# Block 0 of a two-block transformer kernel: convolution by channel halves, layer-norm sums earlier, layer-norm root on GpSimd

## The chip, the cores and the metric

The kernel runs on one core of a Trainium2 chip. The metric is the device time of one execution in microseconds. The kernel before took 1688.28 us (median of three runs, 1686.38 to 1688.96). All engines of the core work side by side and meet only at semaphores: PE (TensorE) does matmuls and transposes, DVE (VectorE) and ACT (ScalarE) elementwise work, POOL (GpSimd) small work and some DMA issues, SP (SyncE) issues the DMAs that bring the weights.

## The reference, cut to what matters

The model is a first part of two layers (a mixer and a mixture of experts with 16 experts in each) and a second part. The change is all in the mixer of layer 0 (`even_mixer`), on 256 tokens:

```
proj = hm @ w_in                       # q 512, k and v 256, u 512, gate 512 columns
attn = block_attention(rope(rms(q)), k, v)        # 8 heads, 128-query blocks, 512 keys
g = u * sigmoid(gate)                             # 512 channels
g = depthwise_conv(g, conv_w) + conv_b            # 31 taps along the tokens
g = silu(layer_norm(g, ln_g, ln_b))               # mean and variance over the 512 channels
out = concat([attn, g]) @ w_out
```

`layer_norm` multiplies the centred rows by `rsqrt(var + 1e-6)`.

## The kernel before, in words

Weights stream from HBM through a ring of eight 2 MB slots. SP issues one DMA for each chunk and waits, for chunk i, until PE has marked chunk i - 8 as used (`chunks_used`). Each engine has one program, written out by hand; nothing is reordered when it runs.

PE's order in the mixer: the u projection (`to_columns`, four channel tiles of 128, eight matmuls each, banks 4 and 5), transposes of the convolution weights (`cw_ps`), the gate projection (banks 6 and 7), q, own k and v, context k and v, one group of modulation chunks (`ada(1, ...)`), transposes of q and k, and then the attention loop of 16 turns, two blocks of eight heads. In turn n PE does the scores of head n + 2 (`ev_scores`, L2059), the transposes of the probabilities of head n (`ev_transposed`, L2067, which waits for the exponential of head n), the products with the values of head n - 1 (`ev_values`, L2074), and one chunk of the modulation weights on average (`ada`, L1875). In turns 10 and 11 (`LN_AT`) it also sums the convolution's output and its squares over the channels with a matrix of ones (`cv_sums`, L2087), in bank 6.

DVE's order: with both sigmoids of ACT there, it multiplies u by them in two instructions (L1284), then runs the convolution as 124 taps (31 for each of four channel tiles), each one instruction of 128x256 (L1297, L1300): 35 (`TAPS_Q`), 12 more after the context's transposes (`TAPS_KV`), and eight in each turn of the loop until none is left. Tap k of all four tiles comes before tap k + 1. Between them stand the norms and rotations of q and k. In turn n of the loop DVE takes the row maximum of head n (L1387), copies transposed probabilities of the even heads (L1393), copies modulation rows (`ada_rows`, L1202), and in turns 10 to 12 does the mean and the centring (`ln_center`), the variance and its reciprocal (`ln_inverse`), and the scaling (`ln_scale`, L1383). ACT takes the exponentials (L689), the squares of the centred rows, and the square root of the reciprocal (L699), for which it loads another function table and then the exponential's again.

POOL stores the modulation gates of groups 1, 2, 4 and 5 to HBM (`store_gate`) as DVE delivers them. `ada_rows(5)` on DVE waits until groups 2 and 4 are stored. A GpSimd power with exponent -0.5 is used at other places for 128x1 and 128x4 operands (L1033, L1062).

After the loop come the output projection (`ev_out`), the routing of layer 0 and then the experts, whose chunks PE takes from the ring.

Of the kernel before, what the change touches and what calls it, by code (L numbers as in the profile page):

```python
# [12 lines left out]
P = 128  # L13
D = 1024
N = 256
# [106 lines left out]
def build(nc, a):  # L122
    ctx = ExitStack()
    with ctx:
# [70 lines left out]
        cw = at(9848, c=CT, j=34)  # L195
        cwrow = at(8824, d=512)
        grow = at(9336, i=P)
# [136 lines left out]
        def whole(eng, name, j=0):  # L334

            used_up(eng, FIRST[name] + j)
# [10 lines left out]
        def pb(b):  # L347
            return ps[:, b, :]
# [51 lines left out]
        SMALL2 = 9  # L400
        LN_AT = 10
        TAPS_Q, TAPS_KV, TAPS_LOOP = 35, 12, 8
        GO = (WO[0], FS)
# [157 lines left out]
        def _(act):  # L561
# [82 lines left out]

            whole(act, "ev_gate")
            for j in range(2):
                nc.scalar.activation(flat(sg[:, 2 * j:2 * j + 2, :]), pb(6 + j), ACT.Sigmoid).then_inc(sem("cv_gate"), 1)

# [7 lines left out]
            for w, bank in ((0, 2), (1, 3)):  # L656
                if w:
                    whole(act, "ev_kv")
                else:
                    act.wait_ge(sem("own_kv"), 1)  # L660
# [24 lines left out]
            for n in range(NT * NQ):  # L685
                act.wait_ge(sem("ev_max"), n + 1)
                if n >= 2:
                    act.wait_ge(sem("ev_pT_ps"), n - 1)
                nc.scalar.activation(pexp[:, n % 2, :], pb(n % 3), ACT.Exp, bias=sm[:, 64 + n:65 + n],  # L689
                                     accum_out=sm[:, 96 + n:97 + n]).then_inc(sem("ev_p"), 1)  # L690
                if n % 2 == 0 and n >= 2:
                    ev_probs_T(n - 1)

                if n == LN_AT:
                    act.wait_ge(sem("cv_centered"), 1)
                    nc.scalar.activation(flat(csq), flat(cacc), ACT.Square).then_inc(sem("cv_sq"), 1)
                if n == LN_AT + 1:
                    act.wait_ge(sem("inverses"), 3)
                    nc.scalar.activation(lnrow[:, :], lnrow[:, :], ACT.Sqrt).then_inc(sem("roots"), 1)  # L699
            ev_probs_T(NT * NQ - 1)  # L700
# [306 lines left out]
        def _(pool):  # L1007
# [31 lines left out]

            for g in (2, 4, 5):  # L1040
                store_gate(g)
# [108 lines left out]
        def _(dve):  # L1150
# [119 lines left out]

            dve.wait_ge(sem("cw_ps"), 1)
            nc.vector.tensor_copy(flat(cw), ps[:, 2, 0:CT * 34]).then_inc(sem("cw"), 1)

            dve.wait_ge(sem("params_in"), PARAMS * 16)
# [5 lines left out]

            whole(dve, "ev_u")
            for j in range(2):
                dve.wait_ge(sem("cv_gate"), j + 1)
                nc.vector.tensor_tensor(gpad[:, 2 * j:2 * j + 2, edge:edge + N],  # L1284
                                        pb(4 + j).rearrange("p (c n) -> p c n", c=2), sg[:, 2 * j:2 * j + 2, :], ALU.mult)\
                    .then_inc(sem("gpad"), 1)

            taps_left = [(k, c) for k in range(CONVK) for c in range(CT)]
            TAPS, tap_of = len(taps_left), {}

            def taps(n):

                for _ in range(min(n, len(taps_left))):
# [9 lines left out]
                    tap_of[c] = TAPS - len(taps_left)  # L1303

            dve.wait_ge(sem("cw"), 1)
            dve.wait_ge(sem("gpad"), 2)
            taps(TAPS_Q)
# [63 lines left out]
            def ln_center():  # L1371
                dve.wait_ge(sem("cv_sum"), 1)
                link(nc.vector.tensor_scalar(lnrow[:, :], ps[:, 6, 0:N], 1.0 / 512, None, ALU.mult))
                nc.vector.tensor_tensor(cacc, cacc, mu, ALU.subtract).then_inc(sem("cv_centered"), 1)

            def ln_inverse():
                dve.wait_ge(sem("cv_sum"), 2)
                link(nc.vector.tensor_scalar(lnrow[:, :], ps[:, 6, N:2 * N], 1.0 / 512, EPS, ALU.mult, ALU.add))
                nc.vector.reciprocal(lnrow[:, :], lnrow[:, :]).then_inc(sem("inverses"), 1)

# [4 lines left out]
            for n in range(NT * NQ):  # L1385
# [13 lines left out]
                if n == NQ + 1:  # L1399
                    attn_rows(0)  # L1400
                if n == LN_AT:
                    ln_center()
                if n == LN_AT + 1:
                    ln_inverse()
                if n == LN_AT + 2:
                    ln_scale()
# [453 lines left out]
        def _(pe):  # L1860
# [57 lines left out]

            def to_columns(i, rhs, banks):

                for c in range(4):
                    for k in range(KD):
                        last = mm(ps[:, banks[c // 2], N * (c % 2):N * (c % 2 + 1)], slot8(i)[:, k, P * c:P * (c + 1)],
                                  rhs[:, k, :], start=(k == 0), stop=(k == KD - 1))
                return last
# [84 lines left out]

            i = FIRST["ev_u"]
            arrived(pe, i)
            used(to_columns(i, xT, (4, 5)))
# [4 lines left out]
            i = FIRST["ev_gate"]  # L2018
            arrived(pe, i)
            used(to_columns(i, xT, (6, 7)))  # L2020
            i = FIRST["ev_q"]
# [7 lines left out]
            pe.wait_ge(sem("cw"), 1)  # L2029
            kv_rows(2, xT).then_inc(sem("own_kv"), 1)  # L2030
            normed_columns("ctx")
# [46 lines left out]
            def cv_sums(n):  # L2078

                if n == 0:  # L2080
                    pe.wait_ge(sem("conv"), CT * CONVK)
                    pe.wait_ge(sem("cleared"), 3)
                    pe.wait_ge(sem("ev_attn"), 2)
                else:
                    pe.wait_ge(sem("cv_sq"), 1)
                for c in range(CT):
                    last = mm(ps[:, 6, N * n:N * (n + 1)], ones[:, 0:P], (cacc, csq)[n][:, c, :],  # L2087
                              start=(c == 0), stop=(c == CT - 1))
                last.then_inc(sem("cv_sum"), 1)
# [3 lines left out]
            for n in range(NT * NQ):  # L2093
                if n + 2 < NT * NQ:
                    ev_scores(n + 2)
                ev_transposed(n)
                if n:
                    ev_values(n - 1)
                if n % 4 == 0 and n:
                    ada_columns(1 + n // 4, 3)  # L2100
                if n in (LN_AT, LN_AT + 1):
                    cv_sums(n - LN_AT)

# [562 lines left out]
```

## Time and profile before

| what | value |
|---|---|
| runs | 1688.96, 1688.28, 1686.38 us |
| the profiled execution | span 1688.5 us, no other time of its own is given with it |
| PE busy | 1483.4 us (88%) |
| DVE busy | 480.6 us (28%) |
| ACT busy | 350.1 us (21%) |
| POOL busy | 112.1 us (7%) |
| DMA | 562.89 MB, mean 333 GB/s |
| mean granted TensorE clock | 0.961 of full speed |

The span runs from the first to the last instruction. Busy shares are averages over very different stages. The mixer of layer 0 lies between 37 and about 217 us, its attention loop between 110 and 191 us, the routing of layer 0 until 243 us, the experts of layer 0 until some 720 us.

### The profile page before, as it was taken

The numbers are of one execution on the slowest core, as the hardware profiler recorded it, in microseconds if no ns is written. First come the engines' busy times: TensorE is split into PE (matmuls) and PEld (weight loads), VectorE is DVE, ScalarE is ACT, GpSimd is POOL, SyncE is SP. The second block draws the span as 40 slices with busy tenths as digits, with TensorE's granted clock in tenths as the row PEclk, the third lists the DMA queues.
The fourth block names the chain that finished last, engine by engine and source line by source line (L and its number), as shares of the span: only waits on it lengthen the run. The fifth ranks groups of instructions, "written<-read, shape, count | busy, mean of one in ns | idle before, by whom it ended". The sixth has DMA issues, their size and how long they took to land. (4 is left out here: it accounts for less than half of the span.)

```text
span 1688.5 us, 18007 instructions
## 1 busy us (share of the span) xinstructions
PE 1483.4 (88%) x7708; PEld 831.6 (49%) x7708; DVE 480.6 (28%) x732; ACT 350.1 (21%) x523; POOL 112.1 (7%) x109
## 2 busy tenths in 40 slices
PE   4999979789888899789798888978878999999999
PEld 2755642232242243289532322323324867788997
DVE  1487540110100000056600100001003765336453
ACT  1122410000000000043210000000003645544442
POOL 0000000000000000010000000000002044330000
PEclk8999979989989999999899999999999999999999
DMA  9979959999999999995489999999999743334520
GB/s 373 375 316 418 396 199 429 416 402 429 416 428 428 413 409 429 415 392 202 168 364 423 427 429 423 428 428 421 429 427 364 271 168 135 121 128 174 198 100 26
DMA packets 93288, 562.89 MB, mean 333 GB/s; under 512 B 8048, under 2 KB 9448, under 8 KB 53670
## 3 DMA queue, kind: packets, MB, share of 16 engines
q1 hardware_dynamic: 89504, 551.77, 80.5%
q0 software_dynamic: 2384, 9.42, 1.6%
q8 instruction: 51, 0.84, 0.2%
q10 hardware_dynamic: 1334, 0.75, 0.2%
q14 instruction: 15, 0.12, 0.0%
HBM read 558.74 MB, written 3.17 MB: 333 GB/s over the span
## 5 line engine op out<-in xcount | busy, mean ns | idle before, releaser
L2211 PE MATMUL ps<-ring,scratch 128*32 128x512 f32 x2048 | 439.0, 609 | 63.0 <-DMA ring<-in_moe_w_up 29.6
L2211 PEld LDWEIGHTS ps<-ring,scratch 128*32 128x32 f32 x2048 | 130.7, 112 | 358.2 <-issue 351.1
L2190 PE MATMUL ps<-ring,scratch 128*32 128x512 f32 x1024 | 206.5, 607 | 28.2 <-DMA ring<-in_moe_w_down 28.2
L1930 PE MATMUL ps<-ring_parts,scratch_parts 128*128 128x512 f32 x656 | 187.0, 402 | 4.9 <-DVE xT_parts L1192 1.4
L1930 PE MATMUL ps<-scratch_parts,ring_parts 128*128 128x256 f32 x704 | 146.5, 281 | 0.0
L1930 PEld LDWEIGHTS ps<-ring_parts,scratch_parts 128*128 128x128 f32 x656 | 122.2, 189 | 33.4 <-DVE xT_parts L1192 1.6
L2190 PEld LDWEIGHTS ps<-ring,scratch 128*32 128x32 f32 x1024 | 50.6, 111 | 159.8 <-issue 109.9
L610 ACT ACTIVATE ring_parts<-ring 128x2048 fp32r<-128x2048 f32 x56 | 106.3, 1917 | 93.1 <-PE ps L1930 86.7
L461 DVE TENSOR_TENSOR ring_parts<-ring,ring_parts 128x2048 fp32r<-128x2048 f32 x46 | 105.7, 2298 | 54.9 <-ACT ring_parts L610 53.7
L1930 PEld LDWEIGHTS ps<-scratch_parts,ring_parts 128*128 128x128 f32 x704 | 116.4, 189 | 0.3
L1523 DVE TENSOR_TENSOR scratch<-ps,gate_bc 128x512 f32<-128x512 f32 x16 | 11.1, 692 | 256.8 <-PE ps L2190 256.8
L1930 PE MATMUL ps<-xT_parts,ring_parts 128*128 128x256 f32 x288 | 82.2, 286 | 1.3 <-DVE xT_parts L1183 1.3
L2219 PE MATMUL ps<-scratch,rows 128*128 128x128 f32 (+1 forms) x256 | 66.6, 421 | 14.1 <-DVE scratch L1552 5.7
L2219 PEld LDWEIGHTS ps<-scratch,rows 128*128 128x128 f32 x256 | 61.5, 327 | 32.1 <-issue 31.0
L1512 DVE TENSOR_TENSOR scratch<-scratch,ps 128x1024 f32<-128x1024 f32 x8 | 9.8, 1221 | 236.7 <-PE ps L2211 236.7
L1915 PE MATMUL ps<-ring,xT 128*128 128x512 f32 x160 | 72.9, 616 | 2.5 <-DVE xT L1171 2.5
L746 ACT ACTIVATE scratch<-ps,mod_cols,scale_cols 128x128 f32<-128x128 f32 x32 | 12.9, 453 | 276.9 <-PE ps L2219 276.9
L1930 PE MATMUL ps<-ring_parts,xT_parts 128*128 128x512 f32 x160 | 62.9, 393 | 0.0
L1508 DVE SCALAR_TENSOR_TENSOR scratch<-ps,cst,scratch 128x256 f32<-128x256 f32 x8 | 3.9, 483 | 186.9 <-ACT scratch L750 186.9
L1875 PE MATMUL ps<-ring,silu_c 128*32 128x512 f32 x384 | 50.0, 656 | 7.8 <-issue 6.9
L758 ACT ACTIVATE scratch<-ps 128x512 f32<-128x512 f32 x8 | 4.8, 597 | 246.7 <-PE ps L2245 246.7
L1930 PEld LDWEIGHTS ps<-xT_parts,ring_parts 128*128 128x128 f32 x288 | 54.2, 188 | 1.8 <-issue 1.5
(394 smaller groups left out, 1574.0 us busy)
## 6 DMA issues: line engine op xcount, KB each, us to landing
ring<-in_moe_w_gate SPq DMA_DIRECT2D x64, 2048.0 KB, 26.2
ring<-in_moe_w_up SPq DMA_DIRECT2D x64, 2048.0 KB, 15.6
ring<-in_moe_w_down SPq DMA_DIRECT2D x64, 2048.0 KB, 27.1
ring<-in_ada_w SPq DMA_DIRECT2D x24, 2048.0 KB, 14.0
ring<-in_mlp_w SPq DMA_DIRECT2D x16, 2048.0 KB, 8.5
ring<-in_sc_w_in SPq DMA_DIRECT2D x6, 2048.0 KB, 21.2
ring<-in_w_in SPq DMA_DIRECT2D x6, 2048.0 KB, 20.0
ring<-in_xattn_wkv SPq DMA_DIRECT2D x4, 2048.0 KB, 27.4
```

The lines of the kernel that those rows point to most:

```text
L461: ops.tensor_tensor(lo, w, hi.bitcast(F32), ALU.subtract).then_inc(sem("w_split"), 1)
L610: nc.scalar.activation(hi, w, ACT.Copy).then_inc(sem("w_high"), 1)
L746: last = nc.scalar.activation(xsT[:, k, :], ps[:, GATHER[b], P * (k % 2):P * (k % 2 + 1)], ACT.Identity, scale=scale[:, k:k + 1], bias=shi ...
L758: nc.scalar.activation(flat(hT[:, 4:8, :]), pb(7), ACT.Copy).then_inc(sem("mo_hT_act"), 1)
L1512: nc.vector.tensor_tensor(hid, hid, ps[:, 2:4, :].rearrange("p b f -> p (b f)"), ALU.mult)\
L1523: nc.vector.tensor_tensor(ym[:, 512 * j:512 * j + 512], pb(4 + j), gate_bc[:, 512 * j:512 * j + 512], ALU.mult).then_inc(sem("mo_ym"), 1)
L1875: last = mm(ps[32 * j:32 * j + 32, bank, :], lhs, rhs, start=(c == k == 0), stop=(c == 3 and k == 1))
L1915: last = mm(ps[:, banks[t], col:col + width], lhs[:, k, P * t:P * (t + 1)], slot8(i)[:, k, 0:width], start=(k == 0), stop=(k == KD - 1))
L1930: last = mm(out, lhs[x], rhs[y], start=start and n == 0, stop=stop and n == 2)
L2190: last = mm(ps[32 * j:32 * j + 32, banks[half], :], src[:, k, CAP * j:CAP * (j + 1)], w[:, e, col:col + 512], start=(k == 0), stop=(k == K ...
L2211: last = mm(ps[32 * j:32 * j + 32, banks[half], :], src[:, k, CAP * j:CAP * (j + 1)], w[e][:, 0, col:col + 512], start=(k == 0), stop=(k = ...
L2219: last = mm(ps[:, GATHER[b], P * (k % 2):P * (k % 2 + 1)], run_slice(rows[:, t, :], k), onehot[:, t, bass.ds(g * P, P)], start=(t == 0), s ...
```

## The change

The u and gate projections are done by channel halves in the order u first half, gate first half, transposes of the convolution weights, u second half, gate second half (`two_columns`). ACT takes the sigmoid of the first half once that half is there, DVE gates it, takes 40 taps of the first two channel tiles (`TAPS_FIRST`), gates the second half, and goes on with 30 and 14 taps; taps now run through the first two tiles before the last two. The ring slot of the u chunk is marked as used after its second half. The mean's sums move to turn 5 of PE's loop, into bank 7, the squares' sums to turn 10. DVE centres in its turn 8, writes variance plus epsilon in its turn 12 (without the reciprocal) and scales in its turn 14. The root and the reciprocal become one GpSimd power of 128x256 elements with exponent -0.5, placed between two gate stores. The convolution's raw weights get another place in SBUF.

```diff
-        LN_AT = 10
-        TAPS_Q, TAPS_KV, TAPS_LOOP = 35, 12, 8
+        TAPS_FIRST, TAPS_Q, TAPS_KV, TAPS_LOOP = 40, 30, 14, 8
+        MEAN_AT, CENTER_AT, SQUARE_AT, VAR_AT, SCALE_AT = 5, 8, 9, 10, 12
...
-            for g in (2, 4, 5):
+            store_gate(2)
+            pool.wait_ge(sem("inverses"), 3)
+            nc.gpsimd.tensor_tensor(lnrow[:, :], lnrow[:, :], mhalf[:, 0:1].broadcast_to([P, N]), ALU.pow)\
+                .then_inc(sem("roots"), 1)
+            for g in (4, 5):
                 store_gate(g)
...
-                if n == LN_AT + 1:
-                    act.wait_ge(sem("inverses"), 3)
-                    nc.scalar.activation(lnrow[:, :], lnrow[:, :], ACT.Sqrt).then_inc(sem("roots"), 1)
...
-            taps_left = [(k, c) for k in range(CONVK) for c in range(CT)]
+            taps_left = [(k, 2 * j + c) for j in range(2) for k in range(CONVK) for c in range(2)]
...
+            gated(0)
...
+            taps(TAPS_FIRST)
+            gated(1)
...
-            def ln_inverse():
+            def ln_var():
                 dve.wait_ge(sem("cv_sum"), 2)
-                link(nc.vector.tensor_scalar(lnrow[:, :], ps[:, 6, N:2 * N], 1.0 / 512, EPS, ALU.mult, ALU.add))
-                nc.vector.reciprocal(lnrow[:, :], lnrow[:, :]).then_inc(sem("inverses"), 1)
+                nc.vector.tensor_scalar(lnrow[:, :], ps[:, 6, N:2 * N], 1.0 / 512, EPS, ALU.mult, ALU.add)\
+                    .then_inc(sem("inverses"), 1)
...
-                if n == LN_AT:
+                if n == CENTER_AT:
                     ln_center()
-                if n == LN_AT + 1:
-                    ln_inverse()
-                if n == LN_AT + 2:
+                if n == VAR_AT + 2:
+                    ln_var()
+                if n == SCALE_AT + 2:
                     ln_scale()
...
+            def two_columns(i, half, rhs, bank):
+                for c in range(2 * half, 2 * half + 2):
...
+            two_columns(u, 0, xT, 4).then_inc(sem("ev_part"), 1)
+            arrived(pe, gate)
+            two_columns(gate, 0, xT, 6).then_inc(sem("ev_part"), 1)
...
+            used(two_columns(u, 1, xT, 5))
+            used(two_columns(gate, 1, xT, 7))
...
+                if n == NQ + 1:
+                    pe.wait_ge(sem("cv_centered"), 1)
...
-                if n in (LN_AT, LN_AT + 1):
-                    cv_sums(n - LN_AT)
+                if n == MEAN_AT:
+                    cv_sums(0)
+                if n == VAR_AT:
+                    cv_sums(1)
```

## Rows read from the trace of the kernel before

**Rows 1.** Stages: window and length in us, busy us (count) by engine, clock, DMA share, GB/s.
```profile
37.20:98.50 61.30, 60.39 (x248) 46.32 (x251) 30.02 (x68) 10.65 (x23) 1.89 (x4) 0.96 0.82 319
...
121.10:191.10 70.00, 69.76 (x504) 35.26 (x500) 43.27 (x91) 22.40 (x43) 1.95 (x5) 1.00 1.02 415
...
226.30:243.00 16.70, 9.78 (x46) 5.55 (x48) 9.87 (x25) 1.68 (x3) 0.00 (x0) 0.57 0.27 82
243.00:820.00 577.00, 507.92 (x2546) 241.69 (x2542) 97.29 (x132) 66.94 (x93) 12.47 (x19) 0.97 0.96 394
```

**Rows 2.** Timeline of SP's DMA issues, 205 to 245 us: start us, us, what.
```profile
243.01 2.08 SPq L496 DMA_DIRECT2D ring<-in_moe_w_up  x2
```

**Rows 3.** Timeline of PE, turns 10 to 15 and the first transposes after them.
```profile
160.71 1.95 PE L2087 MATMUL ps<-scratch,ones 128*128 128x256 f32 x8
...
184.98 0.66 PE L2067 MATMUL ps<-cst,scratch 128*128 128x128 f32 x4
185.47 1.00 PE L2074 MATMUL ps<-scratch 128*128 128x64 f32 x8
186.41 3.64 PE L1875 MATMUL ps<-ring,silu_c 128*32 128x512 f32 x32
...
192.17 1.09 PE L2115 MATMUL ps<-cst,xT 128*128 128x128 f32 x8 [1.09 <-DVE xT L1362]
```

**Rows 4.** Timeline of DVE, turns 11 to 15 and the last modulation rows.
```profile
169.66 0.42 DVE L1378 TENSOR_SCALAR ln_row<-ps 128x256 f32<-128x256 f32 x1 [4.09 <-PE ps L2087]
...
173.26 0.69 DVE L1202 COPY scratch<-ps 128x512 f32<-128x512 f32 x1 [0.84 <-PE ps L1875]
173.87 1.22 DVE L1383 TENSOR_TENSOR scratch<-scratch,ln_row 128x1024 f32<-128x1024 f32 x1
...
177.67 0.69 DVE L1387 TENSOR_REDUCE small<-ps 128x1 f32<-128x512 f32 x1 [0.29 <-PE ps L2059]
...
190.12 0.69 DVE L1202 COPY scratch<-ps 128x512 f32<-128x512 f32 x1 [7.89 <-PE ps L1875]
```

**Rows 5.** Groups of POOL by shape: shapes xcount | busy us, mean ns | idle us.
```profile
L1033 POOL TENSOR_TENSOR rstd<-ms,mhalf 128x1 f32<-128x1 f32 x18 | 11.9, 660 | 1.5
...
L1121 POOL TENSOR_TENSOR scratch<-scratch,small 128x512 f32<-128x512 f32 x2 | 2.1, 1042 | 0.2
L1062 POOL TENSOR_TENSOR small<-small,mhalf 128x4 f32<-128x4 f32 x2 | 2.1, 1040 | 0.2
```

**Rows 6.** All instructions of L1033: ns min/median/max, first and last start us.
```profile
L1033 POOL TENSOR_TENSOR rstd<-ms,mhalf x18: 539/552/2467, 17.9 to 1506.8; 128x1 f32<-128x1 f32 x18
```

**Rows 7.** Timeline of ACT, the exponential of turn 15.
```profile
178.75 0.68 ACT L689 ACTIVATE scratch<-ps,small 128x512 f32<-128x512 f32 x1
179.32 0.20 ACT L689 ACTIVATION_READ_ACCUMULATOR scratch<-ps,small 128x1 f32 x1
```

**Rows 8.** Timeline of PE, turns 0 and 1.
```profile
115.18 1.12 PE L2067 MATMUL ps<-cst,scratch 128*128 128x128 f32 x4 [2.05 <-ACT scratch L689]
...
117.83 3.50 PE L1875 MATMUL ps<-ring,silu_c 128*32 128x512 f32 x16
```

**Rows 9.** The stretch at the lower clock inside it, columns as in rows 1.
```profile
114.23:121.06 6.83, 5.88 (x28) 3.13 (x28) 6.83 (x18) 2.05 (x5) 0.09 (x1) 0.50 1.02 420
```

**Rows 10.** Timeline of POOL, storing and loading a modulation gate.
```profile
113.76 0.56 POOL L1024 DMA_DIRECT2D gate_bc<-gate_scratch  x1 [5.07 <-DMA gate_scratch<-scratch]
```

**Rows 11.** Timeline of DVE, taps before the loop and the first head norm.
```profile
71.75 12.36 DVE L1297 SCALAR_TENSOR_TENSOR scratch<-scratch 128x256 f32<-128x256 f32 x31
...
85.84 4.84 DVE L1297 SCALAR_TENSOR_TENSOR scratch<-scratch 128x256 f32<-128x256 f32 x12
91.53 1.49 DVE L1316 TENSOR_TENSOR rows<-scratch 128x1280 f32<-128x1280 f32 x1 [0.85 <-ACT scratch L666]
```

**Rows 12.** SP's issues of L471, 53 to 75 us: starts, and time to landing.
```profile
L471 SPq DMA_DIRECT2D ring<-in_ada_w x2: 368/368/368, 53.9 to 68.3; - x2
...
DMA to landing us min/median/max: 15.5/20.2/24.9
```

More of the change, by code:

```diff
@@ L195, in build @@
         cw = at(9848, c=CT, j=34)
-        cwrow = at(8824, d=512)
+        cwrow = at(5632, d=512)
         grow = at(9336, i=P)
@@ L643, in _ @@
             act.dma_start(glam[:, :], a["cst_i"]).then_inc(sem("first_params_in"), 16)
-            whole(act, "ev_gate")
             for j in range(2):
+                if j:
+                    whole(act, "ev_gate")
+                else:
+                    act.wait_ge(sem("ev_part"), 2)
                 nc.scalar.activation(flat(sg[:, 2 * j:2 * j + 2, :]), pb(6 + j), ACT.Sigmoid).then_inc(sem("cv_gate"), 1)
@@ L659, in _ @@
                 else:
-                    act.wait_ge(sem("own_kv"), 1)
+                    act.wait_ge(sem("ev_part"), 3)
                 for t in range(NT):
@@ L692, in _ @@
                     ev_probs_T(n - 1)
-                if n == LN_AT:
+                if n == SQUARE_AT:
                     act.wait_ge(sem("cv_centered"), 1)
                     nc.scalar.activation(flat(csq), flat(cacc), ACT.Square).then_inc(sem("cv_sq"), 1)
-                if n == LN_AT + 1:
-                    act.wait_ge(sem("inverses"), 3)
-                    nc.scalar.activation(lnrow[:, :], lnrow[:, :], ACT.Sqrt).then_inc(sem("roots"), 1)
             ev_probs_T(NT * NQ - 1)
@@ L1269, in _ @@
             normed("ctx", ctx_rows, ctx_rows)
-            dve.wait_ge(sem("cw_ps"), 1)
-            nc.vector.tensor_copy(flat(cw), ps[:, 2, 0:CT * 34]).then_inc(sem("cw"), 1)
             dve.wait_ge(sem("params_in"), PARAMS * 16)
@@ L1279, in _, with gated @@
             link(nc.vector.memset(gpad[:, :, edge + N:PADW], 0.0))
-            whole(dve, "ev_u")
-            for j in range(2):
+            def gated(j):
+                if j:
+                    whole(dve, "ev_u")
+                else:
+                    dve.wait_ge(sem("ev_part"), 1)
                 dve.wait_ge(sem("cv_gate"), j + 1)
@@ L1303, in taps @@
                     tap_of[c] = TAPS - len(taps_left)
+            gated(0)
+            dve.wait_ge(sem("cw_ps"), 1)
+            nc.vector.tensor_copy(flat(cw), ps[:, 2, 0:CT * 34]).then_inc(sem("cw"), 1)
             dve.wait_ge(sem("cw"), 1)
+            dve.wait_ge(sem("gpad"), 1)
+            taps(TAPS_FIRST)
+            gated(1)
             dve.wait_ge(sem("gpad"), 2)
@@ L1372, in ln_center @@
                 dve.wait_ge(sem("cv_sum"), 1)
-                link(nc.vector.tensor_scalar(lnrow[:, :], ps[:, 6, 0:N], 1.0 / 512, None, ALU.mult))
+                link(nc.vector.tensor_scalar(lnrow[:, :], ps[:, 7, 0:N], 1.0 / 512, None, ALU.mult))
                 nc.vector.tensor_tensor(cacc, cacc, mu, ALU.subtract).then_inc(sem("cv_centered"), 1)
-            def ln_inverse():
+            def ln_var():
                 dve.wait_ge(sem("cv_sum"), 2)
-                link(nc.vector.tensor_scalar(lnrow[:, :], ps[:, 6, N:2 * N], 1.0 / 512, EPS, ALU.mult, ALU.add))
-                nc.vector.reciprocal(lnrow[:, :], lnrow[:, :]).then_inc(sem("inverses"), 1)
+                nc.vector.tensor_scalar(lnrow[:, :], ps[:, 6, N:2 * N], 1.0 / 512, EPS, ALU.mult, ALU.add)\
+                    .then_inc(sem("inverses"), 1)
             def ln_scale():
@@ L1400, in _ @@
                     attn_rows(0)
-                if n == LN_AT:
+                if n == CENTER_AT:
                     ln_center()
-                if n == LN_AT + 1:
-                    ln_inverse()
-                if n == LN_AT + 2:
+                if n == VAR_AT + 2:
+                    ln_var()
+                if n == SCALE_AT + 2:
                     ln_scale()
@@ L1917, in to_rows @@
                 return last
-            def to_columns(i, rhs, banks):
-                for c in range(4):
+            def two_columns(i, half, rhs, bank):
+                for c in range(2 * half, 2 * half + 2):
                     for k in range(KD):
-                        last = mm(ps[:, banks[c // 2], N * (c % 2):N * (c % 2 + 1)], slot8(i)[:, k, P * c:P * (c + 1)],
+                        last = mm(ps[:, bank, N * (c % 2):N * (c % 2 + 1)], slot8(i)[:, k, P * c:P * (c + 1)],
                                   rhs[:, k, :], start=(k == 0), stop=(k == KD - 1))
@@ L2009, in kv_rows @@
                 return last
-            i = FIRST["ev_u"]
-            arrived(pe, i)
-            used(to_columns(i, xT, (4, 5)))
+            u, gate = FIRST["ev_u"], FIRST["ev_gate"]
+            arrived(pe, u)
+            two_columns(u, 0, xT, 4).then_inc(sem("ev_part"), 1)
+            arrived(pe, gate)
+            two_columns(gate, 0, xT, 6).then_inc(sem("ev_part"), 1)
             pe.wait_ge(sem("params_in"), PARAMS * 16)
@@ L2017, in _ @@
             last.then_inc(sem("cw_ps"), 1)
-            i = FIRST["ev_gate"]
-            arrived(pe, i)
-            used(to_columns(i, xT, (6, 7)))
+            used(two_columns(u, 1, xT, 5))
+            used(two_columns(gate, 1, xT, 7))
             i = FIRST["ev_q"]
@@ L2029, in _ @@
             pe.wait_ge(sem("cw"), 1)
-            kv_rows(2, xT).then_inc(sem("own_kv"), 1)
+            kv_rows(2, xT).then_inc(sem("ev_part"), 1)
             normed_columns("ctx")
@@ L2082, in cv_sums @@
                     pe.wait_ge(sem("cleared"), 3)
+                    pe.wait_ge(sem("cv_gate"), 2)
+                else:
                     pe.wait_ge(sem("ev_attn"), 2)
-                else:
                     pe.wait_ge(sem("cv_sq"), 1)
                 for c in range(CT):
-                    last = mm(ps[:, 6, N * n:N * (n + 1)], ones[:, 0:P], (cacc, csq)[n][:, c, :],
+                    last = mm(ps[:, 7 - n, N * n:N * (n + 1)], ones[:, 0:P], (cacc, csq)[n][:, c, :],
                               start=(c == 0), stop=(c == CT - 1))
```

## Prediction

> **What bounds the kernel now.** I read the stages first [rows 1]. From 37.2 us to the end of the attention loop PE is the bound: 60.39 of 61.30 us busy before the loop, 69.76 of 70.00 in turns 2 to 15. The memory system is busy too (share 1.02 in the loop) but it is not what PE waits for, or PE would show idle time. In the routing, from 226.3 to 243.0 us, the DMA share falls to 0.27: the ring is full, and SP issues the next chunk only at 243.01 [rows 2], when the first expert chunk has been used. From there to 820 us the share is 0.96. So the moment at which PE reaches the experts starts a stretch that the DMA paces, and whatever the mixer gains or loses before 243 us passes to the end one for one. The question is thus when the loop ends, and the place to look is its last turn: transposes of head 15 at 184.98, two modulation chunks at 186.41, DVE's copy of them at 190.12, the next transposes at 192.17 [rows 3, 4].
>
> **Front part, by halves.** PE does the same matmuls in another order, so its sum stays. The gate's first half is ready where u was ready before, at about 53.9 us (SP's release of the u slot, [rows 12]). I allow 2.0 us for the sigmoid, the gating and the weights' copy (no row; an estimate), so taps start near 55.9. Before, the 31 taps from 71.75 on and four more ahead of them came first then. One tap costs 12.36/31 = 0.40 us [rows 11]. 40 taps end at 55.9 + 16.0 = 71.9, gating again 0.7, 30 taps end at 84.6, the context's copies (85.84 - 84.11 = 1.7) at 86.3, 14 taps at 91.9. The head norm started at 91.53 [rows 11], so it comes 0.4 us later. The last thing that PE takes from this chain is the transposes of k, and they stand behind eight transposes of q, some 1.1 us by the eight in [rows 3]; that covers it. I cost it at 0, at most 0.4. The earlier slot release is lost: u's slot comes free after 61 us instead of 53.9. Its DMA landed 24.9 us after its issue, the next one's 15.5 [rows 12]: it sat in a queue, so 7 us of delay are hidden. Cost 0; without that cover, up to 7.
>
> **The loop's taps.** 84 taps are done before the loop instead of 47, so 40 are left, five turns, instead of 77, ten turns. DVE has 5 x 3.2 us less to do in turns 5 to 9. PE was busy throughout these turns [rows 1], so this is worth 0.2 us at most, PE's idle time there (70.00 - 69.76).
>
> **The sums.** Two groups of eight matmuls, 1.95 us each [rows 3]. One moves from turn 11 to turn 5, turns 5 to 11 run 1.9 us later, turn 12 is back in place. Its input, all 124 taps, is ready at the end of DVE's turn 4; ahead of the sums PE transposes head 5, and for that DVE must have taken the maximum of head 5, which comes after those taps: no wait. PE's wait for the centring in turn 9 and DVE's two centring instructions (0.42 + 1.22) before the maximum of head 9 may cost 0.3 us. Behind that wait stand the values of head 8 and the rest of PE's turn. The ACT table changes go, off the path: their end left PE 0.2 us idle, which is the 0.2 already counted. Together: -0.2 to +1, I take +0.3.
>
> **The power on GpSimd.** This is the term that matters. The trace shows the same operation at 128x1 and at 128x4 only. 128x1 takes 0.552 us in the median [rows 6] (the mean, 0.660, has an outlier of 2.467 in it), 128x4 1.040 [rows 5]. Three more elements per partition cost 0.488 us, 0.163 each. 256 elements: 0.552 + 255 x 0.163 = 42.0 us. Other ends: if a power cost in bulk what a multiply costs, 128x512 in 1.042 us [rows 5], it would be 0.9 us with the power's start; if the whole of the 128x4 instruction scaled (0.26 for each element), 66.6 us. The bulk rate isn't shown: a loop over many elements could overlap what a loop of four can't. I take 42, an estimate from the two power sizes, as they are the only rows of this operation, and keep 0.9 and 66.6 as the ends.
>
> Who waits. `ada_rows(4)` starts at 173.26 and takes 0.69, `ln_var` behind it 0.42 like L1378 [rows 4]; with 0.3 from the sums and 0.1 for the semaphore the power starts at 174.8 and ends at 216.8. DVE reaches `ln_scale` in its turn 14, about 178, and stands there. Queued behind it on DVE are the maximum of head 15, the copy of head 14's transposed probabilities, `ada_rows(5)` and `attn_rows(1)`. ACT's exponential of head 15 waits for the maximum, PE's transposes of head 15 for the exponential, and behind them stand the values of head 14 and the last two modulation chunks. After the power: scaling 1.22, maximum 0.69 [rows 4], exponential 0.68 + 0.20 [rows 7], some 0.2 of semaphores: PE transposes at 219.8 instead of 184.98 [rows 3]. That is 34.8 us. In general the delay is the power's length less 7.2 us: up to 7.2 us DVE, ACT and PE hide it.
>
> POOL's queue: `store_gate(4)` stands behind the power, is issued at 216.8, and takes about a microsecond to issue and 5.07 us to land [rows 10], 223. `ada_rows(5)` waits for it; it comes after 3.64 us of chunks [rows 3] that start near 222 at the lower clock, so near 227. Hidden. `store_gate(5)` isn't late relative to the rest. SP: the chunks waiting for the last two modulation slots are issued late, too, but by the same 35 us; the ring is full at the routing as before, since chunk 37 had 16.7 us to spare [rows 1].
>
> **The clock.** A PE that stood idle for 35 us resumes at the lower level. A shorter idle time, in turns 0 and 1, was followed by 6.83 us at a granted clock of 0.50 (1.2 GHz), with 5.88 us of PE work in it [rows 9]; the transposes took 1.12 us instead of 0.66, 16 modulation matmuls 3.50 where 32 took 3.64 at full clock [rows 3, 8]. Half of 5.9 is 2.9 us lost. Between 0 (the clock stays) and 5.3 (the 3.64 us of chunks and 1.66 us of transposes and values at half speed).
>
> **Sum.** 0 (front) + 0.3 (sums) are in the power's start; 34.8 + 2.9 = 37.7 us. The profiled execution gives only its span, 1688.5 us, which is 0.2 above the median of the runs, 1688.3; the trace holds nothing outside the span that the change touches. 1688.3 + 37.7 = 1726 us.
>
> **Rivals.**
> A. The power is cheap in bulk. Where: at `ln_scale`. It decides from 7.2 us, some 27 ns an element: with a shorter power nothing waits, and the time is 1688.3 + 0.3, about 1688.5, not slower. For it: POOL's multiply does an element in 2 ns [rows 5]. Against it: the two power sizes differ by 163 ns an element. The Trainium skill, GPSIMD Engine Reference, section 3.1 (Elementwise, side-by-side cycle accounting), has about 2.6 cycles of 1.2 GHz an element for two-input work, whatever the operation; by that the power would take about 0.6 us, an estimate, and this rival would hold. The trace agrees with the rule for the multiply and not for the power. 11%.
> B. The power costs half as much in bulk, 82 ns an element, 21 us: delay 21 - 7.2 + 2.9 = 17, time 1705. For it: the 128x1 instruction takes 0.552 us, more than three elements' worth, so start and rate can't be parted exactly from two sizes. 17%.
> C. Dearer, up to 66.6 us: 59.4 + 2.9 = 62, time 1750. 4%.
> D. Faster: DVE's relief in turns 5 to 9 and earlier taps gain something. It would need more than 3.4 us; PE's idle time is 0.9 us before the loop and 0.24 in it [rows 1], and the 2.05 us in turn 1 [rows 8] stay, as eight taps stay there. The low clock behind them (2.9 us) would have to go as well. 1684. 2%.
> That the change doesn't do what it says: the taps would have to end later than PE's turn 5; with 40 left they can't.
>
> **How the numbers follow.** The forecast, 1726, holds with 66% (a power of 35 to 48 us, 1719 to 1732). About 0.2% (3.4 us) is what a measurement of this kernel tells from no change. Slower by more needs a power over 10.6 us, or 8 with the clock's loss: 66 + 17 + 4 = 87%, less 1 for the cheap end of B, is 86. Within it: 11% and the 1. Faster: 2%. The range leaves out A, D, the cheap half of B's spread below 1700, and C: 1700 to 1734.
>
> **What would show it.** One POOL instruction of L1042 or near it, TENSOR_TENSOR on ln_row 128x256, of about 42 us from 175 us on; DVE idle before the scaling (38 us) with POOL as what ended it; PE idle before the transposes of head 15 for 34 us; a lower clock for some 7 us afterwards; the first expert chunks issued near 281 instead of 243.01 us; taps starting at 56 us and ending in turn 4; turn 12 of the loop in its old place. Wrong it is if the power takes under 10 us: then only the front and the loop are left, and the time is that of before. A delay in the front, if the head norm starts over a microsecond late and the loop with it, would be the other miss.

## The result, and the profile after

The changed kernel takes 1723.74 us (median of four runs, 1721.8 to 1724.46), the kernel before 1687.86 beside it (four runs, 1686.38 to 1688.96): 35.9 us slower, ratio 1.0218, 95% interval 1.0204 to 1.0231, which is 34 to 39 us. The prediction was 1726, range 1700 to 1734. The profiled execution took 1723.58 us, its span is 1721.8, so 1.8 us lie outside the span; the span of before is 1688.5.

In the page's busy times only POOL's moved by much, from 112.1 us:

```profile
PE 1478.5 (86%) x7708; PEld 831.3 (48%) x7708; DVE 478.7 (28%) x731; ACT 347.4 (20%) x520; POOL 152.8 (9%) x110
```

The 40.7 us are one new instruction of 41.16 us; the other rows of POOL differ by fractions of a microsecond. What the view of its line has on it, with who waited:

```profile
L1042 POOL TENSOR_TENSOR ln_row<-ln_row,mhalf x1: 41158/41158/41158, 173.3 to 173.3; 128x256 f32<-128x256 f32 x1
its engine sat idle before it (us, times) until:
  DVE ln_row L1389: 39.8, 1
who waited for it (us, times):
  DVE scratch L1394: 38.6, 1
```

The timeline of POOL, DVE, ACT and PE behind it (start us, us, what, in brackets the idle time before and what ended it), lines that answer to [rows 3, 4, 7]:

```profile
214.46 1.03 POOL L1019 DMA_DIRECT2D gate_scratch<-scratch  x2
214.52 1.22 DVE L1394 TENSOR_TENSOR scratch<-scratch,ln_row 128x1024 f32<-128x1024 f32 x1 [38.57 <-POOL ln_row L1042]
215.67 0.68 DVE L1398 TENSOR_REDUCE small<-ps 128x1 f32<-128x512 f32 x1
...
216.38 0.69 ACT L692 ACTIVATE scratch<-ps,small 128x512 f32<-128x512 f32 x1 [38.96 <-DVE small L1398]
...
217.22 1.12 PE L2079 MATMUL ps<-cst,scratch 128*128 128x128 f32 x4 [33.59 <-ACT scratch L692]
218.12 1.81 PE L2086 MATMUL ps<-scratch 128*128 128x64 f32 x8
...
219.86 5.02 PE L1886 MATMUL ps<-ring,silu_c 128*32 128x512 f32 x32
...
224.81 1.10 PE L2086 MATMUL ps<-scratch 128*128 128x64 f32 x8
224.96 0.69 DVE L1206 COPY scratch<-ps 128x512 f32<-128x512 f32 x1 [8.01 <-PE ps L1886]
...
227.00 1.09 PE L2132 MATMUL ps<-cst,xT 128*128 128x128 f32 x8 [1.09 <-DVE xT L1373]
```

The chain is power, scaling, maximum of head 15, exponential, transposes. DVE stood idle for 38.57 us, but PE's 33.59 is what counts, since PE had work left when DVE stopped. DVE's copy at 224.96 shows 8.01 us of idle before PE as in [rows 4] (7.89): the gate's store behind the power was in time.

The clock and the memory system in the same stretch (columns as in rows 1; PE idle, the stretch of low clock, from there to the first expert chunk, the experts):

```profile
183.60:217.20 33.60, 0.02 (x3) 0.00 (x0) 2.42 (x3) 0.78 (x2) 31.89 (x3) 0.57 0.35 144
188.56:222.69 34.13, 5.47 (x28) 3.32 (x32) 2.42 (x3) 5.07 (x7) 26.93 (x3) 0.50 0.19 81
222.70:277.80 55.10, 42.79 (x234) 32.14 (x228) 32.75 (x59) 17.03 (x26) 4.77 (x9) 0.85 0.52 184
277.80:820.00 542.20, 471.45 (x2354) 211.95 (x2351) 74.77 (x105) 56.18 (x86) 12.43 (x19) 0.97 0.99 408
```

The clock stood at the lower level from 188.56 to 222.69, 5.47 us of work with it. SP's issue of the first chunk that waits for an expert's is the line that answers to [rows 2]:

```profile
277.78 9.45 SPq L496 DMA_DIRECT2D ring<-in_moe_w_up  x4
```

277.78 - 243.01 = 34.8 us late. That is PE's idle time (33.6) and the loss at the low clock (2.6, worked out below), less the 1.2 us by which this execution was ahead when its loop began, which would be 35.0. The spans differ by 33.3; 1.5 us are given back among the experts of layer 0. The reason was not tested; the two executions have low-clock stretches of different length there.

The front part (DVE, then SP's release of the u slot):

```profile
56.06 15.13 DVE L1302 SCALAR_TENSOR_TENSOR scratch<-scratch 128x256 f32<-128x256 f32 x38
...
85.37 5.62 DVE L1302 SCALAR_TENSOR_TENSOR scratch<-scratch 128x256 f32<-128x256 f32 x14
...
90.92 1.48 DVE L1327 TENSOR_TENSOR rows<-scratch 128x1280 f32<-128x1280 f32 x1
...
60.20 7.28 SPq L471 DMA_DIRECT2D ring<-in_ada_w  x2
```

Taps start at 56 us, the head norm at 90.92. No idle time stands before it any more ([rows 11] had 0.85): DVE has just become the later one there. PE's loop began 1.2 us earlier than in the profile before, because the low-clock stretch in its first projection was shorter in this execution: the granted clock from 37 to 46 us is 0.81, in the profile before 0.69. One later profile of a kernel with the new front (the scaling after the loop and the store first, below) has 0.69 there, too, and its loop begins where the one before began, at 108.75 instead of 108.72 us. There the new front cost PE nothing.

It is not free in every execution, though. In six of the nine profiles with the new front PE's first projection ended 1.0 to 1.8 us earlier than here, and PE then waited 0.74 to 1.34 us before the transposes of k. None of the four profiles with the old front has that wait. From the front part alone:

```profile
105.84 0.66 PE L2058 MATMUL ps<-cst,scratch 128*128 128x128 f32 x4 [0.74 <-DVE scratch L1337]
```

### The profile page after: what moved, and what is told of

Its sections match the earlier page's. It is cut to its first block and busy times, and to the rows that moved or that the text cites. A ratio compares the mean times of both kernels' runs of the same rounds, so it can differ in the third digit from the quotient of the medians.

```text
span 1721.8 us, 18008 instructions
## 1 busy us (share of the span) xinstructions
PE 1478.5 (86%) x7708; PEld 831.3 (48%) x7708; DVE 478.7 (28%) x731; ACT 347.4 (20%) x520; POOL 152.8 (9%) x110
## 5 line engine op out<-in xcount | busy, mean ns | idle before, releaser
L2207 PEld LDWEIGHTS ps<-ring,scratch 128*32 128x32 f32 x1024 | 50.3, 111 | 161.9 <-issue 108.0
L1941 PE MATMUL ps<-ring_parts,rows_parts 128*128 128x512 f32 x160 | 52.7, 398 | 1.6 <-DVE ring_parts L461 1.4
```

The lines of the kernel that those rows point to most:

```text
L1941: last = mm(out, lhs[x], rhs[y], start=start and n == 0, stop=stop and n == 2)
L2207: last = mm(ps[32 * j:32 * j + 32, banks[half], :], src[:, k, CAP * j:CAP * (j + 1)], w[:, e, col:col + 512], start=(k == 0), stop=(k == K ...
```

## The experiments

Each time is compared with the kernel before, run beside it on the same chip. Its medians are 1685.6 us (for the power alone, the sizes, 32 and 96 columns), 1686.0 (root on ACT, front alone, 128x2, no taps first) and 1685.6 (scaling after the loop, store first, no taps first on the kernel before). Its single executions lie between 1681.6 and 1691.2 us. Ratio and interval are those of the comparison; they differ from the quotient of the two medians by up to 0.15%, 2.5 us, and where that matters both are given. The code is cut, and relative to the kernel that the heading names.

**The power alone (on the kernel before).**

```diff
-                if n == LN_AT + 1:
-                    act.wait_ge(sem("inverses"), 3)
-                    nc.scalar.activation(lnrow[:, :], lnrow[:, :], ACT.Sqrt).then_inc(sem("roots"), 1)
...
+            pool.wait_ge(sem("inverses"), 3)
+            nc.gpsimd.tensor_tensor(lnrow[:, :], lnrow[:, :], mhalf[:, 0:1].broadcast_to([P, N]), ALU.pow)\
+                .then_inc(sem("roots"), 1)
...
-                nc.vector.reciprocal(lnrow[:, :], lnrow[:, :]).then_inc(sem("inverses"), 1)
```

> The kernel before with one part of the change alone: reciprocal and square root become the GpSimd power of 128x256, all else stays (sums in turns 10 and 11, scaling in DVE's turn 12, 47 taps before the loop). Theory 1 (the power is the whole cost, and the delay is its length less what the place of the scaling hides): the power starts near 170.2 us, ends near 211.4; scaling, maximum of head 13 and exponential follow, PE transposes head 13 at 214.4 instead of 177.56, 36.8 us late, and 2.9 us go to the lower clock: 1687.9 + 39.7 = 1727.6 us. Theory 2 (halves and earlier sums cost or gain something of their own, and the power only part of the 36 us): clearly below 1724 or above 1731.

Measured 1727.8 us (1726.92 to 1728.84), ratio 1.0242, interval 1.0217 to 1.0267. The power runs 41.16 us. This kernel scales in DVE's turn 12, like the one before, so PE's wait stands before the transposes of head 13:

```profile
207.88 1.23 DVE L1384 TENSOR_TENSOR scratch<-scratch,ln_row 128x1024 f32<-128x1024 f32 x1 [37.41 <-POOL ln_row L1039]
...
210.57 1.11 PE L2068 MATMUL ps<-cst,scratch 128*128 128x128 f32 x4 [36.81 <-ACT scratch L689]
```

One part of the change makes its whole loss. By the waits it loses a little more here: with the scaling two turns later the changed kernel hides 41.16 - 33.59 = 7.6 us of the power, here it is 41.16 - 36.81 = 4.4. The intervals of the two ratios overlap, so the times alone don't show that difference.

**Without the power (on the changed kernel): root back on ACT.**

```diff
-            pool.wait_ge(sem("inverses"), 3)
-            nc.gpsimd.tensor_tensor(lnrow[:, :], lnrow[:, :], mhalf[:, 0:1].broadcast_to([P, N]), ALU.pow)\
-                .then_inc(sem("roots"), 1)
...
+                nc.vector.reciprocal(lnrow[:, :], lnrow[:, :]).then_inc(sem("inverses"), 1)
...
+                if n == VAR_AT + 3:
+                    act.wait_ge(sem("inverses"), 3)
+                    nc.scalar.activation(lnrow[:, :], lnrow[:, :], ACT.Sqrt).then_inc(sem("roots"), 1)
```

> The changed kernel with the root back where it was: reciprocal on DVE in turn 12, square root on ACT in turn 13, scaling in turn 14; halves, taps and sums as changed. Theory 1 (the power is the whole loss, and the rest is hidden behind PE): 1687.9 us, between 1686.5 and 1689. Theory 2 (halves and early sums gain, and the power hid it): under 1684.5. Theory 3 (they cost): over 1691.

Measured 1687.86 us (12 runs), ratio 1.0005, interval 0.9992 to 1.0019. Halves, taps and early sums together are worth nothing that can be told from zero (-1.3 to +3.2 us). Undoing the power gives the 36 us back.

**The front part alone (on the kernel before): halves, 40, 30 and 14 taps; sums in turns 10 and 11.**

```diff
-        TAPS_Q, TAPS_KV, TAPS_LOOP = 35, 12, 8
+        TAPS_FIRST, TAPS_Q, TAPS_KV, TAPS_LOOP = 40, 30, 14, 8
...
+            two_columns(u, 0, xT, 4).then_inc(sem("ev_part"), 1)
+            arrived(pe, gate)
+            two_columns(gate, 0, xT, 6).then_inc(sem("ev_part"), 1)
...
```

> The kernel before with the front part of the change alone: projections and gating by halves, 40, 30 and 14 taps; sums, root and scaling as before. Theory 1: DVE has nothing to do for 15 us in turns 5 to 9 and PE takes no notice, 1687.9 +- 1 us. Theory 2 (the later release of the u slot or the head norm costs): up to 7 us more, 1689 to 1695.

Measured 1685.53 us, ratio 0.9991, interval 0.9977 to 1.0005. The 1687.9 +- 1 written down stood on a kernel before at 1687.9; it ran at 1686.0 here. From 120 to 186 us, the kernel before, then this one:

```profile
120.00:186.00 66.00, 65.78 (x466) 33.01 (x458) 43.67 (x93) 17.34 (x37) 1.95 (x4) 0.99 1.02 415
```

```profile
120.00:186.00 66.00, 65.78 (x478) 33.52 (x480) 27.77 (x53) 19.91 (x39) 1.94 (x4) 1.00 1.02 415
```

DVE has 27.77 us of work instead of 43.67, and PE is as full as before, 65.78 us. An engine that wasn't awaited was given less to do.

**Sizes of the power (instructions added to the kernel before, on data of no use).**

```diff
+            tv = sil[:, :, :].rearrange("p k v -> p (k v)")
+            link(nc.gpsimd.memset(tv, 1.5))
+            for k in (1, 2, 4, 8, 16, 64, 128, 256):
+                link(nc.gpsimd.tensor_tensor(tv[:, 0:k], tv[:, 0:k], mhalf[:, 0:1].broadcast_to([P, k]), ALU.pow))
+            link(nc.gpsimd.tensor_tensor(tv[0:16, 0:256], tv[0:16, 0:256], mhalf[0:16, 0:1].broadcast_to([16, 256]), ALU.pow))
+            link(nc.gpsimd.tensor_tensor(tv, tv, mhalf[:, 0:1].broadcast_to([P, 256]), ALU.mult))
+            link(nc.gpsimd.tensor_tensor(tv, tv, ones[:, :], ALU.pow))
```

> The kernel before with powers of 1, 2, 4, 8, 16, 64, 128 and 256 elements per partition, a power of 16 partitions x 256, a multiply and a power with a full second operand, all on GpSimd behind the norm of the routing, on data that is of no use elsewhere. Theory 1 (a fixed part and a constant rate): 0.4 + 0.16 us for each element, so 0.55, 0.7, 1.04, 1.7, 2.95, 10.6, 20.8 and 41.2 us, and the 16 partitions take as long as 128, since each partition has its own lane. Theory 2 (time goes with all elements): the 16-partition power takes an eighth, 5 us. The multiply near 0.6 us. The stretch of 79 us of powers stands ahead of POOL's gate load, which DVE waits for, so the time is some 70 to 80 us longer.

The groups of POOL by shape (columns as in rows 5):

```profile
L1050 POOL TENSOR_TENSOR silu_c<-silu_c,ones 128x256 f32<-128x256 f32 x1 | 41.2, 41231 | 0.1
L1047 POOL TENSOR_TENSOR silu_c<-silu_c,mhalf 128x256 f32<-128x256 f32 x1 | 41.1, 41115 | 0.1
L1048 POOL TENSOR_TENSOR silu_c<-silu_c,mhalf 16x256 f32<-16x256 f32 x1 | 41.1, 41105 | 0.1
L1047 POOL TENSOR_TENSOR silu_c<-silu_c,mhalf 128x128 f32<-128x128 f32 x1 | 20.7, 20725 | 0.1
L1047 POOL TENSOR_TENSOR silu_c<-silu_c,mhalf 128x64 f32<-128x64 f32 x1 | 10.5, 10519 | 0.1
L1047 POOL TENSOR_TENSOR silu_c<-silu_c,mhalf 128x16 f32<-128x16 f32 x1 | 2.9, 2893 | 0.1
L1047 POOL TENSOR_TENSOR silu_c<-silu_c,mhalf 128x8 f32<-128x8 f32 x1 | 1.6, 1634 | 0.1
L1047 POOL TENSOR_TENSOR silu_c<-silu_c,mhalf 128x4 f32<-128x4 f32 x1 | 1.0, 1012 | 0.1
L1047 POOL TENSOR_TENSOR silu_c<-silu_c,mhalf 128x1 f32<-128x1 f32 x1 | 1.0, 993 | 0.1
L1047 POOL TENSOR_TENSOR silu_c<-silu_c,mhalf 128x2 f32<-128x2 f32 x1 | 0.7, 708 | 0.1
...
L1049 POOL TENSOR_TENSOR silu_c<-silu_c,mhalf 128x256 f32<-128x256 f32 x1 | 0.6, 612 | 0.1
```

From 128 to 256 elements it is 20.390/128 = 0.159 us an element, from 4 to 16 it is 1.881/12 = 0.157: a straight line from 2 elements to 256, with nothing saved in bulk. The single power of one element is off it, 0.993 us where 0.55 was expected; it was the first of the row, and [rows 6] has one such reading, too (2.467 against a median of 0.552). What makes them long wasn't tried. 16 partitions take as long as 128. A power with exponent 1.0, given as a full operand, takes as long as one with -0.5. The multiply of the same shape takes 0.612 us, one 67th. Theory 1 holds. The whole kernel, run once, took 1841.6 us, 156 more, where 70 to 80 were written down: that sum left the 16-partition power and the last power out, 82 us of the 163.

**A shorter power (on the changed kernel): 32 and 96 columns.**

```diff
-            nc.gpsimd.tensor_tensor(lnrow[:, :], lnrow[:, :], mhalf[:, 0:1].broadcast_to([P, N]), ALU.pow)
+            nc.gpsimd.tensor_tensor(lnrow[:, 0:96], lnrow[:, 0:96], mhalf[:, 0:1].broadcast_to([P, 96]), ALU.pow)
```

> The changed kernel with the power on 32 of the 256 columns only; the other columns keep the variance in place of its inverse root. Theory 1: the power takes 0.39 + 32 x 0.159 = 5.5 us, under the 7.2 us that are hidden; DVE may wait 1 to 2 us in turn 14, PE nowhere: 1687 to 1689 us. Theory 2 (a wait on GpSimd costs as such, or the store behind it): above 1691.

> The changed kernel with the power on 96 of the 256 columns only; the other columns keep the variance. Theory 1: 0.39 + 96 x 0.159 = 15.7 us, less 7.2 hidden is 8.5 us of delay at PE's transposes of head 15; if PE's clock falls in this shorter idle time another 2.6: 1696 to 1699 us. Theory 2 (delay in proportion to the power's length, nothing hidden): 15.7/41.2 of 36 us, 13.7: 1701.6 us.

Both kernels leave the root out for the other columns, so what they compute is not the layer, and only their times are of use. 32 columns: 1685.71 us, ratio 0.9999 (0.9986 to 1.0011); PE did not wait for the scaling at all. The median is below the 1687 to 1689 written down, as the kernel before is here at 1685.6 and not at 1687.9. Its power and DVE's wait:

```profile
174.20 5.45 POOL L1042 TENSOR_TENSOR ln_row<-ln_row,mhalf 128x32 f32<-128x32 f32 x1 [39.77 <-DVE ln_row L1389]
179.68 1.23 DVE L1394 TENSOR_TENSOR scratch<-scratch,ln_row 128x1024 f32<-128x1024 f32 x1 [2.87 <-POOL ln_row L1042]
```

96 columns: 1699.33 us, just above the 1696 to 1699 written down. The ratio, 1.0069 (1.0044 to 1.0094), makes that 11.6 us (7 to 16), the two medians 13.8. Its timeline:

```profile
173.34 15.66 POOL L1042 TENSOR_TENSOR ln_row<-ln_row,mhalf 128x96 f32<-128x96 f32 x1 [39.77 <-DVE ln_row L1389]
...
191.72 1.11 PE L2079 MATMUL ps<-cst,scratch 128*128 128x128 f32 x4 [8.10 <-ACT scratch L692]
192.63 1.80 PE L2086 MATMUL ps<-scratch 128*128 128x64 f32 x8
194.36 5.98 PE L1886 MATMUL ps<-ring,silu_c 128*32 128x512 f32 x32
```

15.66 - 8.10 = 7.6 us hidden, the same as with the long power. So the delay is the power's length less 7.6 us. To it come 3.6 us of low clock (5.98 for the chunks where [rows 3] has 3.64, and 1.2 in the two before them), where I had put 2.6. 8.1 + 3.6 = 11.7 lies well within the interval. A delay in proportion to the length would be a wait of 12.8 us (33.59 x 15.66/41.16); the time alone couldn't tell it from theory 1, PE's wait of 8.10 rules it out.

**Where the scaling stands (on the changed kernel).** First the scaling behind `attn_rows(1)`, then also the store of gate 4 ahead of the power.

```diff
-                if n == SCALE_AT + 2:
-                    ln_scale()
...
             attn_rows(1)
+            ln_scale()
```

> The changed kernel, power kept, with the scaling moved from DVE's turn 14 to behind the attention's last rows (after the loop). Theory 1 (who waits, as in the prediction): the loop itself runs through, heads 14 and 15 lose nothing, but the store of gate 4 stands behind the power on POOL, and DVE's last modulation rows wait for it: issue at 214.5, landed some 6 us later, 220.5; attention rows and scaling until 223.5; then Silu on ACT and the split, first product of the output projection near 227 instead of 230.5 in the changed kernel: 1719 to 1723 us, hardly better. Theory 2 (only the maximum of head 15 waits on the power): the loop's end is not touched by POOL, and the time falls to about 1714.

> As the run with the scaling after the loop, and the store of gate 4 put ahead of the power on POOL. Theory 1: nothing but the scaling waits now: the power ends near 215.5, scaling, Silu, high and low parts until some 220, where the first product of the output projection starts (195.3 in the kernel before), 25 us late, and 3 us of clock: 1714 to 1717 us. Theory 2 (the store was no wait): the same time as the run with the scaling after the loop.

1718.44 us (ratio 1.0189, 1.0174 to 1.0203) and 1716.85 us (1.0176, 1.0161 to 1.0192). DVE and PE of the first, then PE of the second:

```profile
217.55 0.69 DVE L1206 COPY scratch<-ps 128x512 f32<-128x512 f32 x1 [35.90 <-DMA gate_scratch<-scratch]
...
219.19 1.97 PE L2131 MATMUL ps<-cst,xT 128*128 128x128 f32 x8 [28.68 <-DVE xT L1373]
```

```profile
221.22 0.77 PE L1940 MATMUL ps<-ring_parts,scratch_parts 128*128 128x512 f32 x1 [26.03 <-DVE scratch_parts L1430]
```

In the first the loop runs through, and the wait that takes the place of the old one is the gate's store behind the power in POOL's queue. The prediction had this wait, and had it hidden behind PE's late chunks; here nothing hides it. The store had landed 2.2 us after its issue at 215.31, not the 5 to 6 that I took from [rows 10], so this run is just under the range written down. In the second only the scaling waits, and 1716.85 is within its range. The intervals of the two overlap; that the store was a wait is shown by the idle time of 35.90 us and its releaser, not by the 1.6 us between the medians. Why the second gains so little can be read: PE's wait fell from 28.7 to 26.0 us only, as the power began 1.1 us later behind the store and Silu and the split follow the scaling.

**The root as a GpSimd power of 128x2 (on the changed kernel).**

```diff
+            nc.gpsimd.tensor_tensor(lnrow[:, 0:NT], lnrow[:, 0:NT], mhalf[:, :], ALU.pow).then_inc(sem("roots"), 1)
...
+                        for c in range(CT):
+                            last = mm(ps[:, 6, N + t:N + t + 1], csq[:, c, P * t:P * (t + 1)], ones[:, 0:1],
+                                      start=(c == 0), stop=(c == CT - 1))
...
+                for t in range(NT):
+                    last = mm(ps[:, 6, P * t:P * (t + 1)], lnrow[:, t:t + 1].broadcast_to([P, P]), ident, start=True, stop=True)
```

> The changed kernel with the root still a GpSimd power, but of 128x2: the squares' sums come out with the tokens on the partitions, the power is taken there, and two matmuls with the identity spread the 256 values over all partitions as a row in PSUM, which the scaling reads in DVE's turn 15. Theory 1 (elements per partition set the power's length): 0.7 us for the power, no wait: 1687 to 1689 us, as with the root on ACT. Theory 2 (GpSimd in the chain costs as such): over 1691.

Measured 1689.93 us, ratio 1.0021 (1.0007 to 1.0034): the 36 us are gone, but it is 3.5 us slower than before, above the range, under the 1691 of theory 2. The power takes 0.72 us and DVE doesn't wait for it. PE has 0.6 us more to do in turn 13, the two matmuls. A part of the rest may lie in the clock. In the profiled execution 16 one-column matmuls at 159.84 were followed by 3.4 us at the lower level (162.6 to 166.0), which cost 1.8 us, half of it here:

```profile
161.67 2.78 PE L1885 MATMUL ps<-ring,silu_c 128*32 128x512 f32 x16
```

instead of 1.92. Whether the one-column matmuls bring it about wasn't tried, and 0.6 and 1.8 don't make up 3.5 us; the cause stays open.

**No taps in DVE's first two turns.** On the kernel with the root on ACT, and on the kernel before (with ten taps a turn).

```diff
-                taps(TAPS_LOOP)
+                if n >= 2:
+                    taps(TAPS_LOOP)
```

> The kernel of the run with the root on ACT, and the 40 taps left moved from DVE's turns 0 to 4 to turns 2 to 6, the mean's sums from turn 5 to 7. In turns 0 and 1 PE waited 2.05 and 0.74 us for exponentials that stood behind taps, and ran 6.8 us at the lower clock afterwards. Theory 1 (these waits are DVE's taps, and the clock follows the waits): up to 2.8 us less, and up to 2.9 more if the clock holds: 1682 to 1685.5 us. Theory 2 (the clock falls for the sparse work before the loop whatever turn 1 does): only the 2 us of waits, some of it again to the low clock, 1686 to 1687. Theory 3: nothing, other waits take their place.

> The kernel before, with no taps in DVE's turns 0 and 1 and ten a turn from turn 2 on (80 places for the 77 left), sums, root and projections as they were. Theory 1 (the gain of the run without taps in the first turns needs the halves): ten taps are 4.0 us, with maximum and copy 5.0 us a turn on the average, over PE's 4.8: what turns 0 and 1 gain is lost in turns 2 to 9: 1685 to 1688 us where the kernel before has 1686. Theory 2 (it comes from the two turns alone): 3 to 5 us faster, as with the halves.

1684.64 us, ratio 0.9977 (0.9963 to 0.9991), and 1682.38 us, ratio 0.9978 (0.9968 to 0.9989). By the ratios both are some 3.8 us faster than the kernel before (1.5 to 6 us), by the medians 1.3 and 3.2. They are the only two versions whose whole interval lies below 1. The gain needs no halves; theory 1 of the second run falls. From 107 to 120 us, the kernel before, then the second:

```profile
107.00:120.00 13.00, 9.82 (x48) 5.69 (x50) 11.06 (x27) 5.19 (x10) 1.80 (x3) 0.78 1.01 422
```

```profile
107.00:120.00 13.00, 12.26 (x80) 5.49 (x76) 11.27 (x25) 4.11 (x10) 0.56 (x1) 1.00 1.01 417
```

PE's wait of 2.05 us in turn 1 [rows 8] is gone and the clock stays up, 80 matmuls are done in the time of 48. In the first of the two the profile shows a low-clock stretch of 6.83 us later, from 188.55; in the second none up to 221 us, and short waits of PE (0.24 to 0.62 us) in its ten-tap turns. That the clock follows this wait is not shown by that. In two of the other profiles (32 columns, and the scaling after the loop) the clock fell ahead of turn 1, at 108.0 and 107.8 us, some 2 us after PE's wait of 1.3 us before the transposes of k, and stayed low for 13.6 us. Of the first:

```profile
108.02:121.66 13.64, 13.03 (x42) 5.39 (x38) 12.59 (x29) 2.87 (x8) 0.56 (x1) 0.50 1.01 419
```

## Why the prediction was right, point by point

**Bound and transmission.** Right within 1.5 us. A delay of 33.6 us in turn 15 plus the clock's share appears as 34.8 us at the first expert chunk and as 33.3 us of span.

**The power.** The term that carried the sum: 42.0 us taken, 41.16 measured. The line through 128x1 and 128x4 had a slope of 0.163 against 0.159. The reservation that bulk might be cheaper, on which rivals A and B lived, is answered by the sizes: it isn't. That the line hit so well has some luck in it. It was drawn 64 times as far as its two points, and a tenth of a microsecond in the first of them is 8 us in the end: with the mean of 128x1 (0.660) in place of the median (0.552) the same sum gives 33 us, and with the single 0.993 that the sizes run has for 128x1 it would give 5. The median of 18 readings was the right choice; a check at one larger size is what makes it safe.

Rival A's mechanism was right in itself (the run with 32 columns: nothing on PE waits), its price was wrong: 0.9 us against 41.16. The Trainium skill (GPSIMD Engine Reference, section 3.1) gives its 2.6 cycles an element for `tensor_tensor` as what reading two inputs costs at least, and the operation that it measured is an add. By that a two-input instruction of 128x256 takes 0.55 us, an estimate; the multiply's 0.612 us is near it and the power's 41.16 isn't. The prediction's "whatever the operation" is more than the page says.

**What hides it.** 7.2 us taken, 7.6 measured twice. From the power's end to the transposes it is 217.22 - 214.49 = 2.7 us where 3.0 was summed. The power's start, 174.8 in the sum and 173.33 in the profile, is earlier mostly for the 1.2 us by which this execution was ahead, and that shifts the end of what hides it as well.

**The clock.** 2.9 us taken. From the transposes of head 15 to the last values' start it is 224.81 - 217.22 = 7.59 us against 189.98 - 184.98 = 5.0 in the kernel before, 2.6. With the power of 96 columns it was 3.6, so this term isn't a constant. After the transposes began, the low level lasted 5.5 us (to 222.69) where some 7 were expected.

**Sum.** 34.8 + 2.9 = 37.7 predicted, 35.9 measured. The traces account for 1.5 of the 1.8 between them: 0.8 is the power's length, 0.4 what hides it and 0.3 the clock. The measured 35.9 is itself known to some 2 us only, so this split is finer than the times can confirm; against the medians of the kernel before in the later comparisons, 1685.6 to 1686.0, it would be near 38. The base of the sum compared a span, 1688.5, with times of whole executions, which are 1.8 us longer; the median that was used is not touched by that.

**Front, taps, sums.** Costed at 0, 0.2 at most, and 0.3. Root on ACT and halves alone give 1.0005 and 0.9991, both with zero inside. The later slot release (60.20 instead of 53.9) was hidden. The front's "at most 0.4" is too small: the eight transposes of q don't cover the later head norm when PE arrives early, and PE waited up to 1.34 us. The times are too coarse to show it. The sums cost nothing: in the profile with the same clock in the first projection as before the transposes of head 15 come at 184.66 instead of 184.98, though the loop began 0.03 later, so +0.3 has the wrong sign.

**Rival D** was right that this change leaves turn 1 as it is (2.06 us of wait in its profile). What I put at 2% as out of reach (the 2.05 us and the clock behind them) was to be had by an edit that the change doesn't make, and gave 3.8 us by the ratios.

## What to carry to other kernels

When an operation moves to another engine, look for rows of that operation on that engine at two sizes and extend the line, then check it at one size near the one that is needed; the price of another operation on the same engine can be off by 67 times, as here. For an engine that works in order, ask which instruction stands behind the wait: the delay is the length less what the place hides. Moving the wait to the end of the loop only brought up the next item of POOL's queue. Work on an engine that isn't awaited was free here, and so was its removal; the taps cost something only in the two turns in which PE waited behind them.

## What the runs showed of the hardware

- A GpSimd power in fp32 costs 0.159 us for each element of a partition, the same with exponent -0.5 as with 1.0 (41.1 and 41.2 us for 256), and the same on 16 partitions as on 128; the multiply of 128x256 takes 0.61 us.
- The stores of a gate from POOL's queue had landed 6.3 us after the first issue in the kernel before (107.45 to 113.76, with the ring's loads under way), and 2.2 us after it in the run with the scaling behind the loop (215.31 to 217.55, with the ring full). Whether the loads make the difference wasn't tried.
- Around turn 1 each of the eleven profiles with taps in DVE's first two turns has a stretch at 1.2 GHz: 3.4 us in three, 6.8 in six, 13.6 in two. In nine it began within PE's wait of 2 us or up to 1.1 us behind its end, in two it began before turn 1; so the wait alone is not shown to be what lowers the clock. The two profiles without those taps, and so without that wait, stay at 2.4 GHz there.
